# The second norm moved into the routing block, and token gathering and combination of a mixture of experts done with exact one-hots in two fp32r passes

## The reference, cut to what matters

```
tok = _modulate(_rmsnorm(xl, norm2_g[l]), sh2, sc2)      # second norm of the layer
s   = sigmoid(tok @ router_w)                            # 32 experts in 4 groups
eidx = top-2 experts inside the best group
wsel = s[eidx] / sum(s[eidx])
# every (token, expert) pair gets a slot, sorted by expert
xb  = tok[tok_buf]                                       # gather
yb  = (silu(xb @ w1[e]) * (xb @ w3[e])) @ w2[e]          # expert
f   = segment_sum(yb * w_buf, tok_buf)                   # combination
xl  = xl + g2 * f
```

## Time and profile before

| what | value |
|---|---|
| median of 3 runs | 3682.86 us (3682.4 to 3685.11) |
| profiled execution | 3683.92 us, its span 3682.1 us |
| PE, DVE, ACT busy | 86%, 55%, 42% of the span |
| mean granted TensorE clock | 0.927 |
| norm 2 and routing, layer 0 | from 1347.5 us to 1461.3 us of the span |
| combination, layer 0 | 2078.1 us to 2156.4 us |
| norm 2 and routing, layer 1 | 3095.7 us to 3144.6 us |
| combination, layer 1 | 3648.4 us to 3672.9 us |

### The profile page before, as it was taken

One profiled execution on the slowest core, in us unless ns is written; L12 is line 12 of the kernel. 1 busy time (PEld: TensorE's weight loads), 2 busy tenths in 40 slices (PEclk: granted clock), 3 DMA queues, 4 the chain that ended last, 5 costly groups with the idle time before them and its releaser, 6 DMA issues. The chain is left out here.

```text
span 3682.1 us, 46697 instructions
## 1 busy us (share of the span) xinstructions
PE 3181.0 (86%) x16830; PEld 2629.1 (71%) x16830; DVE 2032.7 (55%) x2961; ACT 1539.1 (42%) x2164; POOL 0.2 (0%) x4
## 2 busy tenths in 40 slices
PE   8987999887886976999999878788768876799998
PEld 6676766565775763888888737776567866699997
DVE  3454645464454732766666345555464444688884
ACT  3222245332332231666666333334333333577773
POOL 0000000000000000000000000000000000000000
PEclk8998999988997978999999988899989988899999
DMA  4111411041211420899999302241052223699994
GB/s 184 69 46 69 168 52 36 21 177 69 69 58 41 176 99 0 330 338 340 338 341 340 128 35 103 99 178 52 23 206 81 81 79 132 263 422 423 422 422 182
DMA packets 76175, 615.88 MB, mean 167 GB/s; under 512 B 9694, under 2 KB 11680, under 8 KB 13472
## 3 DMA queue, kind: packets, MB, share of 16 engines
q1 hardware_dynamic: 76064, 614.43, 43.4%
HBM read 613.34 MB, written 1.05 MB: 167 GB/s over the span
## 5 line engine op out<-in xcount | busy, mean ns | idle before, releaser
L167 PE MATMUL ps<-rounded,rounded 128*128 128x256 f32 (+1 forms) x1936 | 676.3, 349 | 115.1 <-DVE rounded L158 94.3
L168 PE MATMUL ps<-rounded,rounded 128*128 128x256 f32 (+1 forms) x1936 | 665.7, 344 | 0.0
L169 PE MATMUL ps<-rounded,rounded 128*128 128x256 f32 (+1 forms) x1936 | 663.7, 343 | 0.0
L158 DVE TENSOR_TENSOR rounded<-low_arena,rounded 128x1024 fp32r<-128x1024 f32 (+3 forms) x302 | 359.2, 1228 | 338.4 <-ACT rounded L154 338.4
L167 PEld LDWEIGHTS ps<-rounded,rounded 128*128 128x128 f32 x1936 | 385.6, 199 | 163.6 <-DVE rounded L158 98.1
L143 PE MATMUL ps<-high_arena 128*128 128x256 f32 (+4 forms) x1488 | 437.0, 453 | 73.0 <-ACT low_arena L1616 16.3
L143 PEld LDWEIGHTS ps<-low_arena,high_arena 128*128 128x128 f32 x4096 | 467.0, 192 | 7.4 <-issue 2.4
L143 PE MATMUL ps<-low_arena,high_arena 128*128 128x128 f32 x4096 | 467.7, 275 | 2.0 <-ACT low_arena L2220 1.3
L154 ACT ACTIVATE rounded<-low_arena 128x1024 fp32r<-128x1024 f32 (+3 forms) x302 | 306.5, 1057 | 353.4 <-PE ps L169 274.2
L143 PEld LDWEIGHTS ps<-high_arena 128*128 128x128 f32 x1488 | 289.5, 208 | 208.7 <-issue 115.6
L2242 DVE TENSOR_TENSOR rounded<-high_arena,rounded 128x1024 fp32r<-128x1024 f32 x256 | 313.3, 1225 | 188.1 <-ACT rounded L2202 167.9
(11 more groups left out here) (317 smaller groups left out, 3625.1 us busy)
## 6 DMA issues: line engine op xcount, KB each, us to landing
high_arena<-in_e_w SPq DMA_DIRECT2D x248, 1024.0 KB, 7.4
high_arena<-in_e_w SPq DMA_DIRECT2D x68, 2048.0 KB, 9.2
low_arena<-in_d_wm SPq DMA_DIRECT2D x48, 1024.0 KB, 4.8
high_arena<-in_d_modlater SPq DMA_DIRECT2D x40, 1024.0 KB, 7.0
low_arena<-in_d_wml SPq DMA_DIRECT2D x32, 1024.0 KB, 4.9
low_arena<-in_d_wh SPq DMA_DIRECT2D x16, 1536.0 KB, 6.7
low_arena<-in_d_wa SPq DMA_DIRECT2D x16, 1536.0 KB, 6.7
low_arena<-in_d_wo SPq DMA_DIRECT2D x8, 1024.0 KB, 4.8
```

What stands on the lines that cost most here:

```text
L158: return v.tensor_tensor(lo, raw, hi.bitcast(F32), ALU.subtract)
L167: pe.matmul(out, l_hi, r_hi, start=(k == 0), stop=False)
L168: pe.matmul(out, l_lo, r_hi, start=False, stop=False)
L169: last = pe.matmul(out, l_hi, r_lo, start=False, stop=(k == n - 1))
```

## The change

`stage_norm2` is gone, and its steps are the first of the routing block's lists. The router product runs channel chunk by channel chunk, each as soon as ACT has finished it, into four banks (two in layer 1).

Gathering: the token rows are kept as a rounded part (ACT, fp32r) and a remainder (DVE, fp32r); the one-hot is written as fp32r, which holds 0 and 1 exactly. Each fp32 matmul becomes two fp32r ones, rounded and remainder.

Combination: the slot weights move from the one-hot to the expert outputs. DVE builds diagonal matrices from destinations and weights, TensorE multiplies them by ones, ACT copies the result, and so each of four quantities (two destinations, two weights) is a row of all tokens on every partition. For each slot chunk DVE finds the slot's weight (two operations with an accumulator, one addition), writes the one-hot `pt` directly, and forms the remainder of the weighted output; ACT rounds the weighted output. TensorE interleaves turning the next chunk with the products of this one, for six output tiles at a time in six banks; the last two tiles follow at the end. The transfer of slot numbers at this place is gone.

```diff
+                for k in range(KC):
+                    pe.wait_ge(normed, (k + 1) * ns)
+                    for i in range(T):
+                        last = pe.matmul(K.ps[:, 4 + i, 0:32], K.H[:, k, t0 + i * P:t0 + i * P + P], rw[:, k, :], ...)
                 for i in range(T):
                     for hf in range(2):
                         n = 2 * i + hf
-                        if n >= 2:
-                            pe.wait_ge(h_copied, n - 1)
+                        if n >= 3:
+                            pe.wait_ge(h_split, n - 2)
                         ...
                 pe.wait_ge(routed, 1)
...
-                    accumulate(pe, K.ps[:, 4 + n % 4, :], lambda i: htok[:, i, d * P:d * P + P],
-                               lambda i: oh[:, i, c * 512:c * 512 + 512], T).then_inc(sorted_, 1)
+                    accumulate(pe, K.ps[:, 4 + n % 4, :], lambda q: (h_hi, h_lo)[q % 2][:, q // 2, d * P:d * P + P],
+                               lambda q: oh[:, q // 2, c * 512:c * 512 + 512], 2 * T).then_inc(sorted_, 1)
```

```diff
# DVE, routing block: after the weights (L2011), ahead of the wait for the counts (L2012)
+                for n in range(2 * T):
+                    v.wait_ge(h_copied, n + 1)
+                    remainder(v, h_lo[:, i, d], turn_bank(n), h_hi[:, i, d]).then_inc(h_split, 1)
                 v.wait_ge(counted, 1)
...
-                for i in range(T):
-                    do(v.tensor_scalar(oh[:, i, :], slot_iota, dest[:, i, 0:1], None, ALU.is_equal))
+                for c in range(A // 512):
+                    at = slice(c * 512, c * 512 + 512)
+                    for i in range(T):
+                        do(v.tensor_scalar(oh[:, i, at], slot_iota[:, at], dest[:, i, 0:1], None, ALU.is_equal))
```

```diff
# DVE, combination block
+                def weigh(c):
+                    v.wait_ge(w_ready, c)
+                    for j, w in enumerate((w_first, w_second)):
+                        v.scalar_tensor_tensor(out=junk[j], in0=rows[:, j, :], scalar=slot_of[:, c:c + 1], in1=rows[:, 2 + j, :], op0=ALU.is_equal,
+                                               op1=ALU.mult, accum_out=w[:, c:c + 1]).then_inc(combine_step, 1)
+                    v.wait_ge(combine_step, 3 * c + 2)
+                    v.tensor_tensor(w_slot[:, c:c + 1], w_first[:, c:c + 1], w_second[:, c:c + 1], ALU.add).then_inc(w_ready, 1)
+                def place(c):
+                    v.tensor_scalar(pt[:, c, :], rows[:, 0, :], slot_of[:, c:c + 1], None, ALU.is_equal).then_inc(combine_step, 1)
+                    v.wait_ge(combine_step, 3 * c + 3)
+                    v.scalar_tensor_tensor(out=pt[:, c, :], in0=rows[:, 1, :], ..., in1=pt[:, c, :].bitcast(F32), ...).then_inc(pt_ready, 1)
+                for c in range(SC):
+                    weigh(c)
+                    place(c)
+                    for n in (2 * c, 2 * c + 1):
+                        v.wait_ge(y_rounded, n + 1)
+                        v.scalar_tensor_tensor(out=y_lo[:, c, at], in0=K.ps[:, n % 2, :], scalar=w_slot[:, c:c + 1], in1=y_hi[:, c, at].bitcast(F32),
+                                               op0=ALU.mult, op1=ALU.subtract).then_inc(y_split, 1)
# TensorE, combination block
+                turn(0)
+                pe.wait_ge(rows_copied, 4)
+                for c in range(SC):
+                    if c + 1 < SC:
+                        turn(c + 1)
+                    pe.wait_ge(pt_ready, c + 1)
+                    pe.wait_ge(y_split, 2 * c + 2)
+                    for d in range(banks):
+                        products(c, d)
+                for d in range(banks, KC):
+                    pe.wait_ge(added, (d - banks + 1) * ns)
+                    for c in range(SC):
+                        products(c, d)
```

More of the change, by code:

```diff
@@ L235, in load_constants @@
         K.first.issue(sp, 6, dst, src)
[L238 to L267, removed]
 def filter_consts(K, l):
@@ L1839, in stage_moe @@
              "padded",
-             "spread", "pt_turned", "pt_copied", "y_turned", "y_copied", "combined", "added", "combine_step", "chain")
-    with stage(nc, *names) as (consts_in, w2_in0, w2_in1, logits, exped, routed, counted, h_turned,
+             "y_turned", "combined", "added", "combine_step", "chain")
+    with stage(nc, *names) as (meaned, rooted, rstd_done, scaled, normed, h_split, slots_ready, rows_made, rows_copied, diags, w_ready, pt_ready, y_rounded, y_split, consts_in, w2_in0, w2_in1, logits, exped, routed, counted, h_turned,
                                h_copied, onehot, gathered, sorted_, starts_turned, starts_ready,
@@ L1971, in do @@
                     ch.wait()
+                v.tensor_scalar(rstd, total, 1.0 / D, EPS, ALU.mult, ALU.add).then_inc(meaned, 1)
+                v.wait_ge(rooted, 1)
+                v.reciprocal(rstd, rstd).then_inc(rstd_done, 1)
+                v.wait_ge(rstd_done, 1)
+                for k in range(KC):
+                    v.tensor_tensor(K.H[:, k, t0:], K.X[:, k, t0:], rstd, ALU.mult).then_inc(scaled, 1)
                 do(v.memset(zero32, 0.0))
@@ L2506, in _ @@
-                pe.wait_ge(y_copied, 2 * SC)
-                pe.wait_ge(pt_copied, SC)
-                for d in range(KC):
-                    if d >= 4:
-                        pe.wait_ge(added, (d - 3) * ns)
-                    accumulate(pe, K.ps[:, 4 + d % 4, 0:nt], lambda c: ytok[:, c, d * P:d * P + P], lambda c: pt[:, c, :],
-                               SC).then_inc(combined, 1)
+                for r in range(4):
+                    pe.wait_ge(diags, r + 1)
+                    pe.matmul(K.ps[:, 2 + r, 0:nt], K.ones, diag[:, r].rearrange("p t n -> p (t n)"), start=True, stop=True).then_inc(rows_made, 1)
@@ new lines, in turn, with products @@
+                def turn(c):
+                    for hf in range(2):
+                        n = 2 * c + hf
+                        if n >= 2:
+                            pe.wait_ge(y_split, n - 1)
+                        for k in range(4):
+                            last = pe.transpose(K.ps[:, n % 2, k * P:k * P + P], ys[:, 4 * hf + k, c * P:c * P + P], K.ident)
+                        last.then_inc(y_turned, 1)
+                def products(c, d):
+                    out = K.ps[:, 2 + d % banks, 0:nt]
+                    for n, y in enumerate((y_hi, y_lo)):
+                        last = pe.matmul(out, y[:, c, d * P:d * P + P], pt[:, c, :], start=(c == n == 0), stop=(c == SC - 1 and n == 1))
+                    if c == SC - 1:
+                        last.then_inc(combined, 1)
```

101 lines of the change are left out of this document (52 added, 49 removed).

## The result

| | before | changed |
|---|---|---|
| median | 3683.41 us (3682.4 to 3685.11, 4 runs) | 3621.31 us (3620.92 to 3623.21, 4 runs) |
| span of the profiled run | 3682.1 us | 3619.1 us |
| mean granted TensorE clock | 0.927 | 0.922 |

The ratio is 0.9832, with a 95% interval of 0.9815 to 0.9849: 62.1 us less, where 65.9 was forecast. The predicted time was 3617, its range 3606 to 3630.

A forecast was written before the change was run, and what follows sets the result against it. Four serial stretches bound the kernel, with TensorE alone at work in the gather. Routing gains 25.3 + 7.9, combinations 29.0 + 4.9, semaphores cost 1.2: 65.9 us off, giving 3617 us, range 3606 to 3630.

The forecast's parts named there:

- gather: Routing's gather: two fp32r products of 0.227 us replace each fp32 matmul; gains 25.8 us (layer 0), 6.4 (layer 1).
- norm merged: Norm inside the routing block: router product starts earlier, at 1.2 GHz; gains 7.9 us (layer 0), 4.5 (layer 1).
- added wait: Routing: transposes wait for DVE's subtractions; loses 6.8 us (layer 0), 3.0 (layer 1); counts' price minus 1 to plus 2.
- one-hots: DVE's one-hots in routing, split by columns: 1.6 us more in layer 0, none in layer 1.
- combination, layer 0: Layer 0's combination: DVE paces eight chunks at 4.05 us, TensorE needing 3.8 to about 4.0; gain 29.0 us.
- combination, layer 1: Layer 1's combination, at half the width: four chunks of 3.1 us each; gain 4.9 us.
- semaphores: Combination stage's end: clearing ten more semaphores costs 0.6 us in each layer, 1.2 together.
- stretches taken as fixed: Code outside the changed stages, notably the expert blocks: length taken as unchanged, 0 us.
- rival 4: Gathers and combinations: each fp32r product costs as much as an fp32 matmul, 0.858 us; about 3812 us, chance 0.03.
- rival 2: Router product in routing runs at the full clock; total 3608 us, chance 0.12.
- rival 1: Combinations: TensorE at 1.2 GHz, row products take 3.4 us more, chunks up to 1 more; about 3627, chance 0.18.
- Rival 3: Combination chunks: DVE's two-source products run at half rate, 0.53 us more each, 16 in all; 3633 us, chance 0.05.

The follow-up runs named there:

- experiment 7: Changed kernel with fp32 products nobody reads added to keep TensorE at work before the gather: 3615.5 us (one run).
- experiment 3: Kernel before with only the norm merged into the routing block and the router product run by channel chunk, gather as before: 3674.82 us, ratio 0.9978.
- experiment 8: Changed kernel with first chunk turned before the row products, start numbers transposed inside the gather, counts ahead of the waiting transposes: 3608.3 us, ratio to before 0.9799.
- experiment 4: Changed kernel with TensorE turning the first slot chunk before the four row products instead of after them: 3615.01 us, ratio to before 0.982.
- experiment 5: Changed kernel with the wait for the start numbers and their transposes moved into the middle of the gather: 3609.72 us (one run).
- experiment 6: Changed kernel without the second accumulating product of each combination chunk (second-choice weight left out): 3613.82 us (one run).
- experiments 2: Changed kernel with the combination block of before, so norm and routing changed alone: 3649.76 us, ratio 0.9907.

## Why the prediction came out as it did

The mechanism was right, and so was the sign of every step that was priced; 62.1 us came of 65.9. By the steps of the prediction, in us (measured by the marks above; where the two traces of a kernel differ, the first one stands; the semaphores are the 0.56 us more between layer 1's last addition and the output transfer, taken twice):

| step | forecast | measured |
|---|---|---|
| gather, layer 0 | +25.8 | +25.6 |
| norm merged, layer 0 | +7.9 | +7.8 |
| added wait, layer 0 | -6.8 | -5.8 |
| one-hots, layer 0 | -1.6 | -1.5 |
| gather, layer 1 | +6.4 | +5.2 |
| norm merged, layer 1 | +4.5 | +4.3 |
| added wait, layer 1 | -3.0 | -2.9 |
| combination, layer 0 | +29.0 | +25.9 |
| combination, layer 1 | +4.9 | +3.0 |
| semaphores, both layers | -1.2 | -1.1 |
| stretches taken as fixed | 0 | +2.3 |
| sum | 65.9 | 62.8 |

The two spans differ by 63.0 us, the medians by 62.1.

**Gather.** 0.227 us for a product held to the third digit (1.81 for eight), so rival 4 is gone. In layer 0 the slow start cost about as much as before, as assumed. In layer 1 that assumption failed: TensorE stood at 1.2 GHz from 3072.50 to 3078.00, over half of the new gather. Of the old one only the first tile was slow (3.26 us from the first product to its copy, 1.72 for each later one), which cost 1.5 us; of the new one it is three tiles (copies 1.71 us apart, then 0.91), and experiment 7 shows what that cost, 10.09 - 7.52 = 2.6 us.

**Norm.** The router product stayed at 1.2 GHz with TensorE the later engine: 7.8 and 4.3 us, and rival 2 happened neither here nor in experiment 3.

**Added wait.** The price was right within its bounds. The counts came out at the full clock, the cheap end of "minus 1 to plus 2". The transposes that delay them also run directly ahead of them; that this is the reason is argued, not shown. Experiments 3 and 8 show the other end: there the counts come earlier, after 1.89 and 5.83 us of idle time, and run slow.

**Combination, layer 0.** The term that was mis-sized is its start. The prediction had the rows ready 5.7 us after DVE's first instruction, with row products of 0.858 each; it was 8.6, with three of the four at about 1.7. This is the row price of rival 1 (3.4 us) at a chance of 0.18, and it came true without its second half: the chunks kept 4.05 us, and the tail took 11.3 where 11.1 was forecast. Experiment 4 removes the 2.9 us with TensorE at work until 0.18 us before the row products; experiment 8, in the same order, removes only 1.2 of them, no more than experiment 5 has without it. The prediction had the evidence in hand, the gather's slow first tile after an idle time, and weighed it as a rival where the row itself should have set the term, between 3.7 and 6.7 us for the row products.

**Who paces the chunk.** DVE, as forecast (experiment 6). TensorE's own need was put at 3.8 to 4.0 and is 3.62, because no time is lost between its groups; the slack is 0.4 us, where the forecast's numbers gave 0.05 to 0.25.

**Rival 3.** The accumulating product took 0.75 us for 512 columns, its read of 0.08 lies inside the distance of 0.67 to the next, and no chunk was longer for it; the earlier trace rows had said so. The Trainium skill, page "Vector Engine (DVE) Microarchitecture Reference", section "Points that are easy to get wrong", has this form at half throughput; by the page, as the prediction read it, a chunk would have been 1.6 us longer in layer 0, and the trace doesn't agree: the form is as fast with the accumulator as without. The page doesn't say which rate is halved. Against the one-operand comparison the two-source product does run at half rate, accumulator or not: 512 columns more cost 0.53 us (1.28 for 1024 columns in the trace of before, 0.75 for 512) against 0.27 (0.75 and 0.48); that was in the forecast.

**Combination, layer 1.** Of the 1.9 us missing, 1.2 are the start (4.8 us from the last expert copy to the first chunk instead of 3.5; its row products ran partly slow), 0.5 the chunk of 3.23 instead of 3.1, in which DVE waits 0.1 us for ACT's rounding, and 0.15 the tail. And the trace that the prediction was made from had its last products slow at the start: in the second trace of before this combination takes 23.4 us, not 25.0, and in experiments 2 and 3, which keep the old code, 23.4 and 23.3. So of this term only 1.4 us are surely the change's.

**What was taken as fixed.** The experts of layer 0 became 2.8 us shorter, from a clock that no longer falls in the first of them. The prediction named "any change of the expert block's length" as something that would make it wrong; it was, in its favour and by luck, and made up for part of the 5 us missing in the combinations. What lies ahead of the change came 2.2 us earlier and the mixer, without its semaphores, took 2.1 more, both within the scatter of these stretches.

## What to carry to other kernels

Exact one-hots let an fp32 product be done as two fp32r products at a quarter of its price each, and where TensorE alone bounds a stage this comes out as computed, but for its start. When a stage shrinks, price its start by the slow rows that follow an idle time of TensorE, since the slow microseconds stay and become a larger share. Giving TensorE something useful to do in that idle time is worth a try, not a sure gain: it brought 2.9 us in layer 0 in experiment 4 and nothing there in experiment 8. And after a new order is in place, look once more at what each queue waits for first: here one wait, for numbers that the gather doesn't need, was worth 12 us in one run, a fifth of the whole change.

## What the runs showed of the hardware that was not expected

- In layer 0 the clock level in a short stretch repeated from one trace of a program to the next: row products of 6.65 and 6.66 us in two traces of one kernel, first expert 22.1 us in two traces of another. In layer 1 it didn't always (counts of 2.34 and 1.30 us in two traces of before). Yet the same four row products took 3.70, 5.40 and 6.65 us in different kernels, and 3.70 and 5.40 behind the same transposes and the same 0.18 us of idle time. The same counts ran at 1.2 GHz (6.2 us) or 2.4 GHz (3.2 us); in before, behind nearly the same work and idle time as in the slow case, they took 4.1.
- A change in one stage made the stage after next, whose code is the same, 2.8 us shorter. In twelve traces its time went with the mean granted clock of the stretch from 8 to 30 us in it (0.84, 0.92 or 1.00). A forecast to the microsecond needs the stretches that aren't touched as well.
- Stretches with unchanged code differ by 1 to 2 us from one execution to the next (mixer of layer 1: 939.3 and 941.5; last combination of before: 25.0 and 23.4), so that a term of 1 or 2 us should rest on two traces.
